# Spare expert tiles under one condition, the combine inside the experts' block, six weight slots for the second block's experts

## The reference, cut to what matters

```python
for e in range(N_EXPERTS):
    hid = jax.nn.silu(h @ w_gate[e]) * (h @ w_up[e])
    y = y + gates[..., e:e + 1] * (hid @ w_down[e])
```

## Time and profile before

| | us |
|---|---|
| median of 3 executions | 1836.62 |
| lowest, highest | 1835.6, 1853.08 |
| the profiled execution, its own time | 1831.05 |
| its span, first to last instruction | 1829.2 |

### The profile page before, as it was taken

One profiled execution on the slowest core, in us unless ns is written; L12 is line 12 of the kernel. 1 busy time (PEld: TensorE's weight loads), 2 busy tenths in 40 slices (PEclk: granted clock), 3 DMA queues, 4 the chain that ended last, 5 costly groups with the idle time before them and its releaser, 6 DMA issues. The chain is left out here.

```text
span 1829.2 us, 21620 instructions
## 1 busy us (share of the span) xinstructions
PE 1402.8 (77%) x7554; PEld 1109.0 (61%) x7554; DVE 776.0 (42%) x1456; ACT 444.4 (24%) x917; POOL 366.3 (20%) x339
## 2 busy tenths in 40 slices
PE   7984699843999705739798999989888639777782
PEld 5764566732999605737797987768666525444441
DVE  3786773234334353766273663655123251111012
ACT  3332121201232213314124242333222211111110
POOL 5420000310110022210331404214333201111101
PEclk9996555876999957969899999989989869898886
DMA  4331030035799133020120211302112268999995
GB/s 177 109 124 39 27 112 0 1 126 239 284 378 375 51 115 109 27 92 1 51 92 25 92 65 63 129 24 92 47 61 78 75 267 293 387 382 382 387 394 203
DMA packets 67115, 273.18 MB, mean 149 GB/s; under 512 B 6096, under 2 KB 15952, under 8 KB 54224
## 3 DMA queue, kind: packets, MB, share of 16 engines
q1 hardware_dynamic: 53456, 234.24, 34.3%
q0 software_dynamic: 6656, 23.07, 4.0%
q10 hardware_dynamic: 6912, 14.69, 2.4%
HBM read 242.55 MB, written 29.43 MB: 149 GB/s over the span
## 5 line engine op out<-in xcount | busy, mean ns | idle before, releaser
L1121 POOL TENSOR_TENSOR block_w_lo<-block_w,block_w_hi 128x512 fp32r<-128x512 f32 (+2 forms) x188 | 239.1, 1280 | 758.0 <-ACT block_w_hi L1107 758.0
L1107 ACT ACTIVATE block_w_hi<-block_w 128x512 fp32r<-128x512 f32 (+2 forms) x188 | 111.7, 610 | 323.1 <-PE dil_bank L226 110.7
L1785 PE MATMUL e_gu<-e_w,e_xT 128*64 128x256 f32 x1024 | 141.5, 438 | 54.3 <-DMA e_w<-in_gu 53.4
L1785 PEld LDWEIGHTS e_gu<-e_w,e_xT 128*64 128x64 f32 x1024 | 92.0, 158 | 95.2 <-issue 73.3
L224 PE MATMUL dil_bank<-block_w_hi,xT_hi 128*128 128x512 f32 x288 | 119.5, 415 | 17.6 <-POOL block_w_lo L1121 17.6
L225 PE MATMUL dil_bank<-block_w_lo,xT_hi 128*128 128x512 f32 x288 | 117.2, 407 | 0.0
L226 PE MATMUL dil_bank<-block_w_hi,xT_lo 128*128 128x512 f32 x288 | 116.9, 406 | 0.0
L1855 DVE TENSOR_TENSOR e_prod<-e_sg,e_gu 128x128 f32<-128x128 f32 x32 | 9.2, 288 | 196.1 <-ACT e_sg L1898 196.1
L224 PEld LDWEIGHTS dil_bank<-block_w_hi,xT_hi 128*128 128x128 f32 x288 | 78.0, 271 | 23.1 <-POOL block_w_lo L1121 18.0
L225 PEld LDWEIGHTS dil_bank<-block_w_lo,xT_hi 128*128 128x128 f32 x288 | 78.3, 272 | 4.9
L226 PEld LDWEIGHTS dil_bank<-block_w_hi,xT_lo 128*128 128x128 f32 x288 | 78.0, 271 | 5.3
(11 more groups left out here) (433 smaller groups left out, 3062.5 us busy)
## 6 DMA issues: line engine op xcount, KB each, us to landing
e_w<-in_gu SPq DMA_DIRECT2D x48, 2048.0 KB, 8.9
e_w<-in_dn SPq DMA_DIRECT2D x48, 1024.0 KB, 22.6
block_w<-in_w_dil SPq DMA_DIRECT2D x9, 2048.0 KB, 8.0
block_w<-in_w_out SPq DMA_DIRECT2D x4, 2048.0 KB, 9.4
block_w<-in_w_gates SPq DMA_DIRECT2D x4, 2048.0 KB, 10.3
slot_rows<-e_y ACTq DMA_DIRECT2D x64, 128.0 KB
w_t<-in_w_in_t SPq DMA_DIRECT2D x15, 512.0 KB, 3.7
slot_rows<-blank SPq DMA_DIRECT2D x12, 512.0 KB, 5.8
```

The costliest lines, as they stand in the source:

```text
L1107: act.activation(wh[:, j % RING, 0:width[i]], k.w[:, slot, c, 0:width[i]], ACT.Copy).then_inc(hi_ready, 1)
L1121: pool.tensor_tensor(wl[:, j % RING, 0:width[i]], k.w[:, (q0 + i) % 2, c, 0:width[i]], wh[:, j % RING, 0:width[i]].bitcast(F32), ALU.subtr ...
L1785: ins = pe.matmul(gubank[b % 2][g * S:(g + 1) * S, 0:2 * FG], xT[b % 2][:, c * S:(c + 1) * S], w1[b][:, w:w + 2 * FG], start=(c == 0), sto ...
```

## The change

- `every_tile`: all spare tiles stand under one condition, `If(used > E)`, on every engine; inside it each still has its own. ACT's `empty` is gone.
- `combine` becomes a class `Combine`, whose parts are called at the end of the experts' streams. POOL waits until `y_out` has the share of the used tiles and then gathers; DVE adds; SP stores the output in block two; ACT's multiplication by ALPHA is moved ahead of the first tile. The gathered rows go to `w1` slots 2 and 3 instead of to tensors of their own.
- `k.xh` and `k.xl` get a scope of their own. Block two's experts have six slots: the fifth and sixth lie in the room of `k.xh` and `k.xl` and in `h2`, and their loads are started by SP in `route`, behind its wait for the stored rows and for `logits_done` 1. The number of slots is taken from the list, and as 32 is not a multiple of 6 the loop runs to tile 29 and two tiles are written out behind it.

```diff
+    def turned_rows(self, ctx, name):
+        self.rows_held = ctx.enter_context(ExitStack())
+        self.xh, self.xl = (self.sb(self.rows_held, f"{name}_{x}", [P, KD, SEQ], F32R) for x in ("hi", "lo"))
...
 def route(..., late=None):
                 sp.wait_ge(k.rows_stored, 16 * TT)
+                if late:
+                    sp.wait_ge(logits_done, 1)
+                    late(sp)
...
-    NT, R = most_tiles(E, S), W_SLOTS
+    NT, R = most_tiles(E, S), len(w1)
+    LOOPS, REST = divmod(E, R)
...
             for b in range(R):
                 tile(0, b, surely)
-            with eng.Fori(1, E // R) as i:
+            with eng.Fori(1, LOOPS) as i:
                 for b in range(R):
-                    tile(i, b, surely if b < R - 1 else perhaps)
+                    tile(i, b, surely if REST or b < R - 1 else perhaps)
+            for b in range(REST):
+                tile(LOOPS, b, surely if b < REST - 1 else perhaps)
 
             def extra(i, b):
                 with eng.If(used > R * i + b):
                     tile(i, b, perhaps)
-                if empty:
-                    with eng.If(used < R * i + (b + 1)):
-                        empty(b)
-
-            with eng.Fori(E // R, NT // R) as i:
+
+            with eng.If(used > E):
+                spare_tiles(eng, extra)
+
+        def spare_tiles(eng, extra):
+            for b in range(REST, R if REST else 0):
+                extra(LOOPS, b)
+            with eng.Fori(LOOPS + (REST > 0), NT // R) as i:
                 for b in range(R):
                     extra(i, b)
...
-                with sp.Fori(1, E // R) as i:
+                with sp.Fori(1, LOOPS) as i:
                     for b in range(R):
                         load(R * i + b, i, b)
-                with sp.Fori(E // R, NT // R) as i:
-                    for b in range(R):
-                        extra(i, b)
-                for b in range(NT % R):
-                    extra(NT // R, b)
-                sp.wait_ge(y_out[0], 16 * STORES * ((NT + 1) // 2))
-                sp.wait_ge(y_out[1], 16 * STORES * (NT // 2))
+                for b in range(REST):
+                    load(R * LOOPS + b, LOOPS, b)
+                with sp.If(used > E):
+                    spare_tiles(sp, extra)
+                if tail.store:
+                    tail.store(sp)
...
                 every_tile(pool, used, tile)
+                pool.wait_ge(y_out[0], 16 * STORES * ((used + 1) // 2))
+                pool.wait_ge(y_out[1], 16 * STORES * (used // 2))
+                pool.sem_inc(tail.stored, 1)
+                tail.gather(pool)
...
                 every_tile(dve, used, tile)
+                tail.add(dve)
...
-                def empty(b):
-                    act.sem_inc(y_out[b % 2], 16 * STORES)
-
                 copy_x(0, 0)
-                every_tile(act, used, tile, empty)
+                if tail.scale_rows:
+                    tail.scale_rows(act)
+                every_tile(act, used, tile)
...
+class Combine:
+    def __init__(self, k, name, out_rows, room, x, scale, out=None, stats=None):
+        self.rows = [room[j // 4][:, j % 4 * DM:(j % 4 + 1) * DM] for j in range(2 * TT)]
...
+    def gather(self, pool):
+        pool.wait_ge(self.stored, 1)
+        for j in range(2 * TT):
+            tt, i = divmod(j, 2)
+            pool.indirect_dma_start(self.rows[j], None, self.out_rows, bass.IndirectOffsetOnAxis(
+                ap=self.k.slot[:, i, tt:tt + 1], axis=0)).then_inc(self.row_in[j], 16)
...
     stage.close()
+    k.rows_held.close()
     k.recycle_semaphores()
     with ExitStack() as s:
         h2 = k.sb(s, "h2_nat", [P, TT, DM])
         weights, router = expert_weights(k, "e2", s), router_weights(k, "r2", G2 + E2, s)
+        w1, w2, w1_in, w2_in = weights
+        more_in = [[k.sem(f"e2_{n}{W_SLOTS + i}") for i in range(2)] for n in ("w1", "w2")]
+
+        def late_loads(sp):
+            for i in range(2):
+                sp.dma_start(more_w1[i], d["gu2"][W_SLOTS + i]).then_inc(more_in[0][i], 16)
+                sp.dma_start(more_w2[i], d["dn2"][W_SLOTS + i]).then_inc(more_in[1][i], 16)
+
+        k.turned_rows(s, "h2T")
...
+        k.rows_held.close()
+        more = k.sb(s, "e2_more_w", [P, KD * 2 * FF + 2 * 2 * DM])
+        more_w1 = [more[:, 0:KD * 2 * FF], h2[:].rearrange("p t n -> p (t n)")]
+        more_w2 = [more[:, KD * 2 * FF + 2 * DM * i:KD * 2 * FF + 2 * DM * (i + 1)] for i in range(2)]
+        route(k, "r2", E2, G2, S2, router, s, d["rows"], lambda tt: h2[:, tt, :], late_loads)
+        weights = ([x[:] for x in w1] + more_w1, [x[:] for x in w2] + more_w2, w1_in + more_in[0], w2_in + more_in[1])
+        experts_moving(k, "e2", E2, S2, k.gather_sems[2:4], d["rows"], d["gu2"], d["dn2"], d["slots"][0:SLOTS2, :], weights,
+                       Combine(k, "c2", d["slots"][0:SLOTS2, :], w1[2:4], k.x1, 1.0, out=d["out"]))
```

More of the change, by code:

```diff
@@ L313, in place_block1 @@
     k.x1 = k.sb(k.ctx, "x_res", [P, TT, DM])
[L315 removed]
     k.row_stats = k.sb(k.ctx, "row_stats", [P, TT, 2, 6])
+    k.turned_rows(k.ctx, "xT")
     k.v = k.sb(ctx, "v1", [P, TT, FEW])
@@ L1197, in first_loads, with route @@
         sp.dma_start(w2[e][:], w_dn[e]).then_inc(w2_in[e], 16)
-def route(k, name, E, G, S, router, ctx, rows, x_store):
+def route(k, name, E, G, S, router, ctx, rows, x_store, late=None):
     nc = k.nc
@@ L1399, in __call__, with experts @@
         return self.eng.If(self.used > t)
-def experts(k, name, E, S, x_in, rows, w_gu, w_dn, out_rows, weights):
+def experts(k, name, E, S, x_in, rows, w_gu, w_dn, out_rows, weights, tail):
     nc = k.nc
@@ L1905, in tile @@
                             take_y(i, b)
-                def empty(b):
-                    act.sem_inc(y_out[b % 2], 16 * STORES)
                 copy_x(0, 0)
[L1911 to L1941, removed]
-                    for i in range(2):
-                        j = 2 * tt + i
-                        dve.wait_ge(row_in[j], row_base[j] + 16)
-                        dve.scalar_tensor_tensor(x[:, tt, :], yr[j][:], k.gate[:, i, tt:tt + 1], x[:, tt, :],
-                                                 ALU.mult, ALU.add).then_inc(used, 1)
-                        dve.wait_ge(used, j + 1)
-                    if stats is not None:
-                        for half in range(2):
-                            step(row_stats(dve, stats[:, tt], x[:, tt, :], half))
-            if out is not None:
-                @block.sync
-                def _(sp):
-                    for tt in range(TT):
-                        sp.wait_ge(used, 2 * tt + 2)
-                        sp.dma_start(out[tt * P:(tt + 1) * P, :], x[:, tt, :]).then_inc(out_done, 16)
-                    sp.wait_ge(out_done, 16 * TT)
-    for j in range(2 * TT):
-        k.gathered[4 + j] += 16
@@ L2320, in second_block @@
         transpose_split(k, "h2T", lambda tt, b: h2[:, tt, b * P:(b + 1) * P], lambda b: (k.xh[:, b, :], k.xl[:, b, :]), KD)
-        route(k, "r2", E2, G2, S2, router, s, d["rows"], lambda tt: h2[:, tt, :])
-        experts_moving(k, "e2", E2, S2, k.gather_sems[2:4], d["rows"], d["gu2"], d["dn2"], d["slots"][0:SLOTS2, :], weights)
-        combine(k, "c2", d["slots"][0:SLOTS2, :], k.x1, 1.0, out=d["out"])
+        k.rows_held.close()
[6 more added lines that the diff above has]
+                       Combine(k, "c2", d["slots"][0:SLOTS2, :], w1[2:4], k.x1, 1.0, out=d["out"]))
 def first_block(k):
@@ L2380, in first_block @@
         route(k, "r1", E1, G1, S1, router, s, d["rows"], lambda tt: k.x1[:, tt, :])
-        experts(k, "e1", E1, S1, k.gather_sems[0:2], d["rows"], d["gu1"], d["dn1"], d["slots"][0:SLOTS1, :], weights)
-        combine(k, "c1", d["slots"][0:SLOTS1, :], k.x1, ALPHA, stats=stats)
+        experts(k, "e1", E1, S1, k.gather_sems[0:2], d["rows"], d["gu1"], d["dn1"], d["slots"][0:SLOTS1, :], weights,
+                Combine(k, "c1", d["slots"][0:SLOTS1, :], weights[0][2:4], k.x1, ALPHA, stats=stats))
     layer_norm(k, "ln2", k.x1, "ln2_g", "ln2_b", stats)
```

55 lines of the change are left out of this document (44 added, 11 removed).

## The result

| us | before | after |
|---|---|---|
| median of 4 executions | 1836.11 | 1877.63 |
| lowest, highest | 1834.87, 1853.08 | 1863.43, 1881.66 |
| the profiled execution, its own time | 1831.05 | 1876.23 |
| its span | 1829.2 | 1874.4 |

The ratio is 1.019 (1.011 to 1.027): slower, outside the range.

A forecast was written before the change was run, and what follows sets the result against it. Block two's experts were taken as bound by the weight stream, with both seams on the path. Seams 6.4 + 6.5, stream 16.3, less 1.5 for the gather: 27.7 us off 1836.6, say 1809; range 1801 to 1820.

The forecast's parts named there:

- the sum: Whole kernel: 6.4 + 6.5 + 16.3 - 1.5 = 27.7 us saved, taken from a median of 1836.6.
- All five rivals: Gather behind late loads 0.10, seams still slow 0.05, loop fetch stalls 0.04, late loads starting late 0.03, slower weight stream 0.03.
- The seams: Between experts and combine: the first gather starts 6.4 us earlier in block one and 6.5 in block two.
- the 5.5 and 4 named: Sign: first combine gather within 5.5 us of block one's last store and 4 us of block two's.
- The two streamed experts: Block two's tiles: 26 experts streamed there instead of 28, at 8.17 us each, saving 16.3 us.
- The first gather: Block two's first token gather meets the end of the late loads: 1.5 us lost, bounds 0 and 3.6.
- The collision rival: Block two: first gather lands behind the late loads, costing 3.6 us, and the second as much; 1815 us, chance 0.10.
- its second half, the second gather: Block two: the second token gather also lands late, costing as much again as the first gather's 3.6 us.
- ALPHA and the loop's body: ACT's 3.89 us multiplication moved ahead of the tiles, and block two's six-tile loop: each forecast to cost 0.
- the stall that its two-page rule would bring: Block two's PE loop: rival of three back jumps at 3.74 us, none covered; 1820 us, chance 0.04.
- low ends: Seams 8, stream 11, first gather -3.6: only 15.4 us saved, so 1821.

The follow-up runs named there:

- after_warm8_early: Changed kernel with eight dense matmuls before each dilated attention, and the fifth expert's load issued before the stored rows land; 1810.0 us, ratio 0.988.
- first_seam_old: Changed kernel with block one's experts and combine put back as they were before, block two as changed; 1853.4, 1889.0, 1889.7 and 1890.7 us.
- before_pause6: Kernel before with one added block of six small chained DVE memsets ahead of the whole dilated part; 1881.4 to 1883.3 us, ratio 1.027.

## Why the prediction was wrong

**The step that failed is what the sum was subtracted from.** The sum took all untouched code at its time in the one profiled execution. It had no term for the granted clock of the three dilated attentions, worth 65 us, and no rival that named it. All five rivals lay within the touched stages. What could have been read: the third time of the kernel before, 1853.08, stood 16.5 us above the others with nothing to explain it (one narrow attention at the low clock costs 17), and block one's attention, thin work like the others, ran at half the clock in the same profile. Three executions were too few to show that the kernel before takes 1855 us and more half of the time.

**The sum itself came nearly true, in part by luck.** With the clock held up in both, the changed kernel is 1843.0 - 1815.7 = 27.3 us shorter side by side, and 1841.8 - 1816.9 = 25.0 at first, on two chips; the forecast was 27.7. But the touched parts gave only 21.7 of it in the traces, and the rest came from code that the forecast held fixed. The parts one by one:

- *The seams.* Forecast 6.4 + 6.5, measured 7.0 + 6.3 in the trace. Right: stores and gathers stood 4.51 and 3.73 us apart, inside the 5.5 and 4 named.
- *The two streamed experts.* Forecast 16.3, the stretch from 271.8 to 255.5. The first streamed load was issued at 1581.83 and the last landed at 1840.4, 258.6 us: 13.2 gone. Right in mechanism, some 3 us too high. The queues of the changed kernel between 1582 and 1838 us (packets, MB, share) say where 2 of them are:

```profile
q1 hardware_dynamic: 7388, 81.12, 83.0%
```

  81.12 MB are 25.8 experts, so one takes 256 x 0.830 / 25.8 = 8.24 us of the engines' time where it took 8.17; over 26 of them 1.8 us. The term held that price fixed.
- *The first gather.* Forecast 1.5 of at most 3.6, measured 4.1, so this term was mis-sized too: the loads were given 17 us from their issue (1493 to 1510) and took 18.7 (1553.71 to 1572.4), and the gather landed behind all of them. Slots and gather together were to bring 14.8 us; the run with four slots gives them 9.1. The collision rival had this half right; its second half, the second gather, isn't seen. In `after_warm8_early` the gather is back at its old pace; the time falls by 3.0 us side by side, within the spread, and by 6.9 at first, on two chips.
- *ALPHA and the loop's body.* Forecast 0, and no stall is seen. With ALPHA's 3.88 us in front ACT still waited 1.96 us for PE ahead of its first `e_sg`, where it had waited 5.71; the table load behind it takes 1.28 us, as it did before the change. The branches of the changed kernel on PE's queue (count: least, middle and longest ns, from, to):

```profile
L1703 PEldq COMPARE_BRANCH  x4: 76/210/241, 1653.1 to 1825.7; - x4
...
L1449 PEldq COMPARE_BRANCH  x1: 3438/3438/3438, 631.0 to 631.0; - x1
...
L1713 PEldq COMPARE_BRANCH  x1: 3940/3940/3940, 1844.8 to 1844.8; - x1
```

  The six-tile loop turns back in 0.24 us at most. The two jumps over the spare code take 3.4 and 3.9 us, as large as the longest before, and end before the first gather: PE has nothing more to do there. The larger room of the Trainium skill (Runtime: NRT & Kernel Launch, Instruction fetch mechanics), 128 KB for PE, is what this loop's branch agrees with; the stall that its two-page rule would bring isn't seen in a body of 588 instructions.
- *The rest.* The traces give 21.7 us to the touched parts and the two comparisons 25.0 and 27.3. Between block one's combine and block two's router, where no instruction is touched, the changed kernel with eight matmuls is 6.0 us (side by side) and 7.7 us (at first) shorter than its partner in the traces. Why wasn't tried; that these gains filled what the slots fell short of is luck.
- *The range.* The forecast's own low ends give 1821 us, and the range was closed at 1820; 1877.6 is outside either.

The Trainium skill says in TensorE: Matmul & The Clock Gate, Part 1, that the number of matmuls at the low clock at a kernel's start is "run-variable", and that the ramp penalty is under 1% of a typical span. No run here measures that ramp. What these runs show is as variable, one program taking both 1833 and 1900 us on one chip, but lies elsewhere and is larger: 65 of 1831 us, 3.5%, paid in the middle and for the whole length of three attentions.

**What stays open.** Why the odds differ by build: the kernel before loses the clock in some attention in half of its executions, the changed kernel lost it in all 12, so with its clock left alone the changed kernel was the slower one. `first_seam_old` and `before_pause6` show that neither the seam nor any code of the change is needed for a loss, and they share no other feature that a run has isolated. Placement of `k.xh` and `k.xl` and the exact length of the stretch ahead (132.8 us from the latent attention's scores to the first dilated ones in the changed kernel, 133.6 to 133.7 before) were not separated; in the kernel before itself an execution with 133.6 kept the clock and one with 133.7 lost it.

## What to carry to other kernels

Before subtracting a gain from a profiled time, look at the granted clock of every stage, also of those that the change doesn't touch: here thin stages at 1.00 behind a barrier could fall to 0.5, and then took two thirds longer. Compare two versions only with that held equal; here eight dense matmuls in front of each attention, 2.1 us an attention, did it, and turned an apparent loss of 41 us into a gain of 25 to 27. Check that gain stage by stage as well: 6 us of it came from stages that nobody had touched. And a small gather that the path waits for loses time when it is issued into the tail of a bulk load, 4 us here; an earlier start of the load gave them back in the traces.

## What the runs showed of the hardware

- In the dilated attentions a fall came within 5 us of the first scores or not at all, and scores at 1.2 GHz (528 ns in the mean) did not bring the clock back in any trace, though PE was busy 99% of the stretch; with one exception the next dense projection did (in `before_pause6` it rose for 3.5 us behind the third attention's last scores). A fall in the first microseconds thus costs all of the stage, 17 us in a stretch of 26.
- The same program on the same chip does either (1833 us at a mean granted clock of 0.85, 1900 at 0.81). A barrier's pause of 1 us in front was there in both cases; 2.5 us of idle PE in its place made it no better. Behind 2.1 us of dense matmuls, 67 of 68 undisturbed executions of five builds showed no loss by their times.
- A gather of 64 rows issued while the weight queue was full took 8.0 to 8.3 us to reach PE, and 3.8 to 4.3 with that queue idle or just running out, although it has a queue of its own.
